# Latent mixers: u projected in pairs, convolution taps beside the projections, the second tile's heads behind the first search

## The chip, the cores and the metric

The kernel runs on one core of one Trainium2 chip. The metric is the device time of one execution in microseconds (us); lower is better. Times are medians of several executions. Everything is float32.

## What is computed

Two blocks of two layers each run one after the other on 256 tokens of width 1024. The change touches the second block only, and in it the two "latent" layers:

```
hx = modulate(x, sh1, s1)
q, k, v, u = split_cols(hx @ w_in[l])
q = apply_rope(rms(q.reshape(B, S, N_Q_HEADS, HEAD_DIM)) * q_gain[l], cos, sin)
k = apply_rope(rms(k.reshape(B, S, N_KV_HEADS, HEAD_DIM)) * k_gain[l], cos, sin)
o_attn = attend_latent(q, jnp.concatenate([kc, k], axis=1), jnp.concatenate([vc, v], axis=1))
o_conv = conformer_conv(u, conv_w[l], conv_b[l], ln_g[l], ln_b[l])
x = x + g1 * merge_groups(o_attn, o_conv, beta_attn[l], beta_conv[l], w_o[l])
x = x + g2 * peer(modulate(x, sh2, s2), peer_wq[l], peer_keys[l], peer_u[l], peer_v[l])
```

`conformer_conv` halves u (1024 columns) into a and gate, takes a * sigmoid(gate), and convolves its 512 channels along the tokens with 31 taps. `peer` picks, for each token and each of 8 heads, 16 of 16384 experts by two searches (best 16 of 128 keys twice, then best 16 of the 256 sums), gathers a row of u and a row of v for each pick, and adds up gelu(h . u) * weight * v.

## The kernel before, in words

Tokens lie in two tiles of 128 (t = 0, 1). Each engine runs one instruction stream written out by hand, and counts in semaphores order them. A latent layer (`stream_pe_in`, then `latent_mixer_pe`, `latent_mixer_act`, `latent_mixer_dve`, then a loop over 256 picks) goes so:

- PE projects q, k, v of both tiles (line 343 under a helper), then u as eight groups of 128 channels j = 0 to 7, where group j of a needs gate group j + 4. ACT reads each from PSUM (L995, identity or sigmoid). DVE meanwhile normalises and rotates q and k (L1303 to L1341) and signals `rot_ready`. PE transposes q and k (L337, "qk"), ACT copies them into `QT` and `KT`.
- DVE multiplies a by the gate in one instruction (L1345) into `PAD`. Then `maximum(i)` (L1436) finds the row maximum of head i's scores, and `taps_at(i)` gives the taps behind it. Each tap k of channel groups 0 to 2 is three DVE instructions (L1354, L1356) and a wait for the last of them (`link`). Group 3's taps are matmuls with diagonal matrices (L790), which POOL builds (L1223).
- The 16 heads (8 per tile) each go score (PE, L780), maximum (DVE), exponential (ACT, L1109), transposes (PE, L798), copy (ACT, L1117), values (PE, L807), with two buffers each. Heads 0 to 12 are begun beside the taps, and 13 to 15 beside the first search.
- Behind the taps: the convolution is transposed (L819), normalised, gated, multiplied by w_o (line 343), and gives h of tile 0 (L1481). PE projects queries and key scores of expert head 0 (L763), DVE searches (`search(0, 0)`, `search(0, 1)`) and writes the first 16 picks to `IDX` (L1650).
- From then on POOL fetches one row pair per pick (L2901), 1 MB each, into one of 15 slots. For pick n DVE takes the dot product (L2846), ACT the gelu and a scaled diagonal (L2787 to L2794), and PE adds the row (L2710). Only then is the slot free. `SLOT_FROM_TO` says for which picks a slot is in use, and in which order slots are first taken. Tables by n hang the rest of the layer (more queries, searches, tile 1's w_o products at n = 12 and 18) into this loop. `free` makes the first use of a slot wait for whoever held the memory, as here for the query and key buffer and for the buffer of the probabilities:

```
SLOT_QKT: [(s.groups_done, groups.of("score", TT * QH - 1))], SLOT_PROBS: [(s.groups_done, groups.of("pv", TT * QH - 1))],
```

Slots `W0A` and `W1A` (picks 24 and 25) wait for tile 1's w_o products in the same way, and POOL takes all fetches in order.

## Time and profile before

| what | us |
|---|---|
| median of 3 runs | 2952.42 |
| lowest, highest | 2946.86, 2974.02 |
| span of the profiled execution | 2910.0 |
| DVE busy in the span | 2101.8 (72%) |
| PE busy in the span | 2441.3 (84%) |
| bytes moved, mean rate | 1038.89 MB, 357 GB/s |

The span runs from the first to the last instruction on the core, so some 42 us of the time lie outside it. In it the first latent layer's projections begin near 1272 us and the second's near 2090 us. In the rows, a start time is counted from the beginning of the span, a bracket at the end holds the idle time of the engine before the instruction and what ended it, and xN is the number of instructions merged into the row. A float32 matmul or transpose shows as two matmul instructions.

### The profile page before, as it was taken

The numbers are of one execution on the slowest core, as the hardware profiler recorded it, in microseconds if no ns is written. First come the engines' busy times: TensorE is split into PE (matmuls) and PEld (weight loads), VectorE is DVE, ScalarE is ACT, GpSimd is POOL, SyncE is SP. The second block draws the span as 40 slices with busy tenths as digits, with TensorE's granted clock in tenths as the row PEclk, the third lists the DMA queues.
The fourth block names the chain that finished last, engine by engine and source line by source line (L and its number), as shares of the span: only waits on it lengthen the run. The fifth ranks groups of instructions, "written<-read, shape, count | busy, mean of one in ns | idle before, by whom it ended". The sixth has DMA issues, their size and how long they took to land.

```text
span 2910.0 us, 27822 instructions
## 1 busy us (share of the span) xinstructions
PE 2441.3 (84%) x8610; PEld 1389.1 (48%) x8610; DVE 2101.8 (72%) x4478; ACT 819.3 (28%) x2274; POOL 1124.6 (39%) x1121
## 2 busy tenths in 40 slices
PE   6996898978898999979798877768797988877876
PEld 3664364756546566656444333324375444332322
DVE  1659479878888978788587777765466977777654
ACT  1231111100012100013443433334324444433443
POOL 1100445766563676461143333334211334333332
PEclk9988897989997899989899899989998999999999
DMA  8348999999999999982499999999831999999997
GB/s 349 144 181 339 369 415 383 374 412 413 416 411 365 402 394 412 395 297 76 191 413 420 420 420 420 420 419 409 351 123 50 414 420 420 420 420 420 420 421 318
DMA packets 183478, 1038.89 MB, mean 357 GB/s; under 512 B 26971, under 2 KB 28978, under 8 KB 99876
## 3 DMA queue, kind: packets, MB, share of 16 engines
q0 software_dynamic: 147456, 805.37, 68.1%
q1 hardware_dynamic: 35292, 230.38, 19.9%
q8 instruction: 70, 1.15, 0.2%
q10 hardware_dynamic: 584, 1.36, 0.1%
q14 instruction: 76, 0.62, 0.1%
HBM read 1032.60 MB, written 4.44 MB: 356 GB/s over the span
## 4 chain that ended last, share of the span: by engine, by line
DMA 33%; PE 31%; DVE 21%; issue 6%; POOL 4%; ACT 3%; SPq 0%; ACTq 0%; DVEq 0%; POOLq 0%
PE PS L343 13%; DMA W<-in_peer_uv,IDX 12%; PE PS L2710 12%; DMA PROJ<-in_peer_uv,IDX 7%; DMA ROWS<-in_peer_uv,IDX 4%; DVE ROWS L1356 4%; DMA ROWS<-in_peer_uv,IDXV 3%; DMA ROWS<-in_peer_uv,COEF 3%; POOL ROWS L2539 2%; DVE ROWS L2331 2%; PE PS L2132 1%; PE PS L2142 1%; DMA ACC<-in_peer_uv,COEF 1%; PE PS L483 1%; DVE PROD L2344 1%
## 5 line engine op out<-in xcount | busy, mean ns | idle before, releaser
L2710 PE MATMUL PS<-W,SCALE 128*128 128x512 f32 x1120 | 539.7, 625 | 99.1 <-ACT SCALE L2794 99.0
L2846 DVE CUSTOM_DVE_ANT_0 W<-W,PS 128x1024 f32<-128x1024 f32 x280 | 337.9, 1219 | 213.5 <-DMA W<-in_peer_uv,IDX 212.9
L2901 POOL DMA_INDIRECT W<-in_peer_uv,IDX x280 | 267.8, 957 | 400.6 <-PE PS L2710 344.9
L2710 PEld LDWEIGHTS PS<-W,SCALE 128*128 128x128 f32 x1120 | 214.2, 199 | 406.0 <-issue 404.9
L2539 POOL DMA_INDIRECT ROWS<-in_peer_uv,IDX x159 | 170.0, 1069 | 366.4 <-DVE IDX L1653 150.5
L2132 PE MATMUL PS<-XT,W 128*128 128x256 f32 x1408 | 307.4, 379 | 0.0
L2132 PEld LDWEIGHTS PS<-XT,W 128*128 128x128 f32 x1408 | 267.8, 190 | 45.5 <-issue 10.1
L2787 ACT ACTIVATE DOT<-DOT 128x1 f32<-128x1 f32 x512 | 103.5, 202 | 602.8 <-DVE DOT L2846 595.9
L343 PE MATMUL PS<-W,XT 128*128 128x512 f32 (+2 forms) x576 | 220.6, 545 | 10.5 <-ACT XT L963 5.7
L343 PE MATMUL PS<-XT,W 128*128 128x128 f32 (+1 forms) x1344 | 218.6, 323 | 3.7 <-ACT XT L1076 3.7
L2794 ACT ACTIVATE SCALE<-C,COEF 128x128 f32<-128x128 f32 x512 | 205.6, 402 | 48.2 <-PE PS L2710 1.4
L343 PEld LDWEIGHTS PS<-XT,W 128*128 128x128 f32 x1344 | 201.0, 194 | 26.8 <-issue 6.7
L2331 DVE CUSTOM_DVE_ANT_0 ROWS<-ROWS,PS 128x1024 f32<-128x1024 f32 x118 | 139.8, 1217 | 42.7 <-DMA ROWS<-in_peer_uv,IDX 40.9
L343 PEld LDWEIGHTS PS<-W,XT 128*128 128x128 f32 x576 | 109.1, 200 | 119.9 <-issue 108.2
L2790 ACT ACTIVATE COEF<-DOT,WGT 128x1 f32<-128x1 f32 x512 | 150.8, 295 | 48.3 <-ACT DOT L2787 0.8
L343 PE MATMUL PS<-W,CT 128*128 128x512 f32 x320 | 150.2, 627 | 6.9 <-ACT CT L1127 4.2
L2901 POOL DMA_INDIRECT ROWS<-in_peer_uv,IDX x44 | 41.6, 946 | 224.2 <-DVE EI L1655 178.9
L2142 PE MATMUL PS<-W,PP 128*128 128x512 f32 x192 | 95.1, 653 | 29.9 <-DVE PP L2499 29.9
L2344 DVE SCALAR_TENSOR_TENSOR PROD<-ROWS,COEF,PROD 128x1024 f32<-128x1024 f32 x80 | 102.7, 1284 | 22.3 <-DMA ROWS<-in_peer_uv,COEF 14.8
L1356 DVE SCALAR_TENSOR_TENSOR ROWS<-ROWS,COLC 128x256 f32<-128x256 f32 x270 | 115.5, 482 | 2.1
L2710 PE MATMUL PS<-ROWS,SCALE 128*128 128x512 f32 x176 | 93.4, 657 | 26.2 <-ACT SCALE L2794 26.0
L2539 POOL DMA_INDIRECT ROWS<-in_peer_uv,COEF x80 | 91.5, 1144 | 43.5 <-DVE PROD L2344 22.4
(422 smaller groups left out, 4066.7 us busy)
## 6 DMA issues: line engine op xcount, KB each, us to landing
W<-in_w_up SPq DMA_DIRECT2D x44, 1024.0 KB, 12.2
W<-in_w_in SPq DMA_DIRECT2D x21, 2048.0 KB, 11.1
W<-in_w_mod SPq DMA_DIRECT2D x7, 4096.0 KB, 12.8
W<-in_w_down SPq DMA_DIRECT2D x22, 1024.0 KB, 8.1
W<-in_peer_wq SPq DMA_DIRECT2D x6, 2048.0 KB, 8.8
W<-in_w_o SPq DMA_DIRECT2D x6, 2048.0 KB, 9.5
W<-in_w_out SPq DMA_DIRECT2D x4, 2048.0 KB, 11.8
ROWS<-in_w_mod SPq DMA_DIRECT2D x5, 1024.0 KB, 12.2
```

The source lines that it names most:

```text
L343: ins = nc.tensor.matmul(PS[:, b, cols[0]:cols[1]], lhs(k), rhs(k), start=start and k == 0, stop=stop and k == n_k - 1)
L1356: ins = nc.vector.scalar_tensor_tensor(B["U"][:, j, :], B["PAD"][:, j, k:k + S], tap, B["U"][:, j, :], ALU.mult, ALU.add)
L2132: ins = nc.tensor.matmul(PS[:, 2 * r + half, j * S:(j + 1) * S], up_half(i, half)[:, k, j * P:(j + 1) * P], XT[:, k, :], start=(k == 0), s ...
L2142: ins = nc.tensor.matmul(PS[:, 4 + 2 * t + n, :], HG[r][:, j, t * P:(t + 1) * P], wslot(2 + r, 2, D)[:, j, n * 512:(n + 1) * 512], start=F ...
L2331: nc.vector.tensor_tensor_reduce(beside_slot(l, m), beside_slot(l, m), h, 1.0, 0.0, ALU.mult, ALU.add, DOT[:, 0, m:m + 1]).then_inc(beside ...
L2344: nc.vector.scalar_tensor_tensor(total, slot, coef, total, ALU.mult, ALU.add).then_inc(beside_used, 1)
L2539: nc.gpsimd.indirect_dma_start(beside_slot(l, n), None, one_by_one, bass.IndirectOffsetOnAxis(index[:, n % PICKS:n % PICKS + 1], 0),).then ...
L2710: ins = nc.tensor.matmul(PS[:, SUMS2[t] + h, :], SCALE[:, n % NSCALE, :], v_of(n)[:, h * 512:(h + 1) * 512], start=m == 0, stop=m == PICKS ...
L2790: nc.scalar.activation(COEF[:, t, one], DOT[:, t, one], ACT.Copy, scale=WGT[:, t, one]).then_inc(s.coef_ready, 1)
L2794: nc.scalar.activation(SCALE[:, n % NSCALE, :], ident, ACT.Copy, scale=COEF[:, t, one]).then_inc(s.scale_ready, 1)
L2846: nc.vector.tensor_tensor_reduce(u_of(n), u_of(n), h_of(t), 1.0, 0.0, ALU.mult, ALU.add, DOT[:, t, m:m + 1]).then_inc(s.rows_used, 1)
L2901: nc.gpsimd.indirect_dma_start(pair_slot(n), None, in_pairs, bass.IndirectOffsetOnAxis(IDX[:, t, m:m + 1], 0),).then_inc(pair_signal(fetch ...
```

## The change

In the latent layers, and there alone:

- PE projects u in the order 0, 4, 1, 5, 2, 6, 3, 7, so that a group and its gate come together, and puts the transposes of q and k behind the sixth group. ACT follows that order, and takes the root for q and k behind one u group in place of two.
- DVE multiplies group by group (`pad`), and does 26 taps ahead of the first maximum: 12 over groups 0 and 1, 14 over groups 0 to 2. Each tap is one instruction on one group. It waits for that group's previous tap, which was never the instruction just before it. The number of DVE taps stays 93.
- Only tile 0's heads (0 to 7) run beside the rest of the taps, in pairs. Tile 1's heads (8 to 15) come behind the first search: their first four maxima lie between the search and pick 0, the others behind picks 0 and 1. ACT and PE do them ahead of pick 0.
- The slots of the query and key buffer and of the probabilities are first used by picks 7 and 8 in place of 4 and 5.

```diff
-(SLOT_ROWS, SLOT_G, SLOT_PROJ, SLOT_KV, SLOT_QKT, SLOT_PROBS, SLOT_W0B, SLOT_W1B, SLOT_W0A, SLOT_W1A,
- SLOT_W2A, SLOT_W2B, SLOT_W3A, SLOT_W3B, SLOT_MORE) = range(15)
-SLOT_FROM_TO = [(0, 72), (0, 180), (0, 256), (0, 180), (0, 256), (0, 180), (0, 256), (0, 256), (24, 256), (24, 256),
-                (76, 256), (76, 256), (76, 256), (76, 256), (0, 256)]
+(SLOT_ROWS, SLOT_G, SLOT_PROJ, SLOT_KV, SLOT_MORE, SLOT_W0B, SLOT_W1B, SLOT_QKT, SLOT_PROBS, SLOT_W0A, SLOT_W1A,
+ SLOT_W2A, SLOT_W2B, SLOT_W3A, SLOT_W3B) = range(15)
+SLOT_FROM_TO = [(0, 72), (0, 180), (0, 256), (0, 180), (0, 256), (0, 256), (0, 256), (0, 256), (0, 180), (24, 256), (24, 256),
...
 NSCALE = 4
-TAP_HEADS = 12
-
-
-def taps_at(i):
-
-    return range(TAPS2 * i // TAP_HEADS, TAPS2 * (i + 1) // TAP_HEADS)
+U_ORDER = (0, 4, 1, 5, 2, 6, 3, 7)
+QK_TURN = 6
+PE_GROUP = 3
+PE_TAPS = (0, 6, 12, 18, 24, TAPS2)
+
+
+def tap_plan(parts):
+
+    done, before, plan = [0] * PE_GROUP, None, []
+    for n, groups in parts:
+        plan.append([])
+        for _ in range(n):
+            free = [g for g in range(groups) if done[g] < TAPS2]
+            g = min(free, key=lambda g: (g == before, done[g], g))
+            plan[-1].append((g, done[g]))
+            done[g], before = done[g] + 1, g
+    assert done == [TAPS2] * PE_GROUP, done
+    return plan
+
+
+TAP_PLAN = tap_plan([(12, 2), (14, 3), (14, 3), (14, 3), (14, 3), (25, 3)])
...
-            for j in range(8):
+            def turn_queries():
+                pe.wait_ge(s.rot_ready, 1)
+                transposes(pe, s, banks, groups, "qk", lambda t, k: B["QR"][:, t, k * P:(k + 1) * P], 6, s.qkT_ready, 0)
+
+            for i, j in enumerate(range(8) if beside else U_ORDER):
                 c = 2 + j // 4
                 if j % 4 == 0:
                     weights_in(pe, s, c, first)
-                b = banks.take(s.conv_in_ready, j + 1)
+                if not beside and i == QK_TURN:
+                    turn_queries()
+                b = banks.take(s.conv_in_ready, i + 1)
                 matmul_rows(pe, b, (0, S), lambda k: wslot(c, DK, 512)[:, k, (j % 4) * P:(j % 4 + 1) * P],
                             lambda k: XT[:, k, :], DK).then_inc(s.groups_done, groups.mark("u", j))
                 groups.at["u", j, "bank"] = b
             if beside:
                 beside(banks, 0)
-
-            pe.wait_ge(s.rot_ready, 1)
-            transposes(pe, s, banks, groups, "qk", lambda t, k: B["QR"][:, t, k * P:(k + 1) * P], 6, s.qkT_ready, 0)
+                turn_queries()
             pe.wait_ge(s.qkT_ready, 3)
...
             banks.leave_out(5)
             banks.hold(5, s.conv_ready, 2)
-            for i in range(TAP_HEADS):
-                score(i)
-                taps(taps_at(i))
-                if i >= 2:
+            for i in range(0, QH + 2, 2):
+                if i < QH:
+                    score(i)
+                    score(i + 1)
+                if i:
                     turn_probs(i - 2)
-                if i >= 3:
-                    sum_values(i - 3)
-            head(12)
+                    turn_probs(i - 1)
+                taps(range(PE_TAPS[i // 2], PE_TAPS[i // 2 + 1]))
+                if i:
+                    sum_values(i - 2)
+                    sum_values(i - 1)
             pe.wait_ge(s.conv_ready, 2)
...
+            banks.read_out[6] = (s.merged_ready, 1)
+            banks.banks, banks.i = [b for b in banks.in_turn() if b not in (2, 3)] + [6], 0
             turn_h(0)
             queries(0, 0)
             key_scores(0, 0)
-            for i in (13, 14, 15):
-                score(i)
             for c in range(2):
                 product("Y", 1, c, s.y_read, 2 + c + 1)
-            for j in (13, 14, 15):
-                turn_probs(j)
-                sum_values(j - 1)
-            sum_values(15)
             queries(0, 1)
             key_scores(0, 1)
-            banks.read_out[6] = (s.merged_ready, 1)
+            score(QH)
+            score(QH + 1)
+            for i in range(QH + 2, TT * QH + 2, 2):
+                if i < TT * QH:
+                    score(i)
+                    score(i + 1)
+                for j in (i - 2, i - 1):
+                    turn_probs(j)
+                for j in (i - 2, i - 1):
+                    sum_values(j)
...
-            exps(13)
...
                 nc.scalar.copy(H[:, 1, c * 512:(c + 1) * 512], PS[:, b, :]).then_inc(s.y_read, 1)
-            exps(15)
-            for j in (13, 14, 15):
-                probs_turned(j)
             queries_in(0, 1)
             scores_in(0, 1)
+            for i in range(QH, TT * QH + 2, 2):
+                if i == QH + 4:
+                    first_softmax()
+                if i > QH:
+                    probs_turned(i - 2)
+                    probs_turned(i - 1)
+                if i < TT * QH:
+                    exps(i)
+                    exps(i + 1)
...
+        def conv_for(dve, s, link, B):
+            step_of = {}
+
+            def pad(g):
+                dve.wait_ge(s.conv_in_ready, 2 * g + 2)
+                nc.vector.tensor_tensor(B["PAD"][:, g, HALO:HALO + S], B["U"][:, g, :], B["U"][:, 4 + g, :], ALU.mult).then_inc(s.pad_ready, 1)
+
+            def taps(part):
+                for g, k in part:
+                    tap = B["COLC"][:, g, k:k + 1]
+                    if k == 0:
+                        dve.wait_ge(s.pad_ready, g + 1)
+                        ins = nc.vector.tensor_scalar(B["U"][:, g, :], B["PAD"][:, g, 0:S], tap, B["COLC"][:, g, TAPS2:TAPS2 + 1], ALU.mult, ALU.add)
+                    else:
+                        dve.wait_ge(s.dve_step, step_of[g])
+                        ins = nc.vector.scalar_tensor_tensor(B["U"][:, g, :], B["PAD"][:, g, k:k + S], tap, B["U"][:, g, :], ALU.mult, ALU.add)
+                    ins.then_inc(s.dve_step, 1)
+                    step_of[g] = link.count.next()
+
+            def taps_done():
+                dve.wait_ge(s.dve_step, link.count.value())
+                dve.sem_inc(s.conv_ready, 1)
+
+            return pad, taps, taps_done
         def context_mixer_dve(dve, s, link, norms, groups, B, SRC):
...
-            for i in range(TAP_HEADS):
+            pad(0)
+            pad(1)
+            taps(TAP_PLAN[0])
+            pad(2)
+            taps(TAP_PLAN[1])
+            pad(PE_GROUP)
+            for i in range(0, QH, 2):
                 maximum(i)
-                for k in taps_at(i):
-                    tap_step(k)
-            maximum(12)
+                maximum(i + 1)
+                taps(TAP_PLAN[2 + i // 2])
+            taps_done()
             merge_heads(0)
...
                     maximum(i)
-            return {"key": last_maxima}, {
-                2: second_heads, 3: second_stat, 7: second_ratio, 16: lambda: add_product("O", 1, 0, ri[:, 0, 2:3]),
+            return {
+                -2: lambda: second_maxima(QH), -1: lambda: second_maxima(QH + 2), 0: lambda: second_maxima(QH + 4),
...
-                    within["key"]()
                     search(0, 1)
+                    later[-2]()
+                    later[-1]()
                     for n in range(TT * PICKS):
                         t, m = divmod(n, PICKS)
```

On PE, from the end of the projections of u of a latent layer into the heads (XT,W is u, C,QR the transposes of q and k, QKT a score, the rows with CT are taps of group 3, C,ROWS and V,ROWS probabilities and values). Before:

```order
L343 MATMUL PS<-XT,W 128x256 x64
L337 MATMUL PS<-C,QR 128x128 x12
L780 MATMUL PS<-QKT 128x512
L790 MATMUL PS<-ROWS,CT 128x256 x2
L780 MATMUL PS<-QKT 128x512
L790 MATMUL PS<-ROWS,CT 128x256 x3
L780 MATMUL PS<-QKT 128x512
L790 MATMUL PS<-ROWS,CT 128x256 x2
L798 MATMUL PS<-C,ROWS 128x128 x4
```

After:

```order
L358 MATMUL PS<-XT,W 128x256 x48
L352 MATMUL PS<-C,QR 128x128 x12
L358 MATMUL PS<-XT,W 128x256 x16
L799 MATMUL PS<-QKT 128x512 x2
L809 MATMUL PS<-ROWS,CT 128x256 x6
L799 MATMUL PS<-QKT 128x512 x2
L817 MATMUL PS<-C,ROWS 128x128 x8
L809 MATMUL PS<-ROWS,CT 128x256 x6
L826 MATMUL PS<-V,ROWS 128x64 x8
```

The transposes of q and k moved ahead of the last two u groups, and scores come two at a time.

On DVE, from the last copy of k and v into the heads. Before:

```order
L1341 COPY V<-KV 128x256
L1345 TENSOR_TENSOR ROWS<-ROWS 128x4x256
L1436 TENSOR_REDUCE NMAX<-PS 128x1
L1354 TENSOR_SCALAR ROWS<-ROWS,COLC 128x256 x3
L1356 SCALAR_TENSOR_TENSOR ROWS<-ROWS,COLC 128x256 x3
L1436 TENSOR_REDUCE NMAX<-PS 128x1
L1356 SCALAR_TENSOR_TENSOR ROWS<-ROWS,COLC 128x256 x9
```

After:

```order
L1366 COPY V<-KV 128x256
L1394 TENSOR_TENSOR ROWS<-ROWS 128x256 x2
L1401 TENSOR_SCALAR ROWS<-ROWS,COLC 128x256 x2
L1404 SCALAR_TENSOR_TENSOR ROWS<-ROWS,COLC 128x256 x10
L1394 TENSOR_TENSOR ROWS<-ROWS 128x256
L1401 TENSOR_SCALAR ROWS<-ROWS,COLC 128x256
L1404 SCALAR_TENSOR_TENSOR ROWS<-ROWS,COLC 128x256 x13
L1394 TENSOR_TENSOR ROWS<-ROWS 128x256
L1486 TENSOR_REDUCE NMAX<-PS 128x1 x2
L1404 SCALAR_TENSOR_TENSOR ROWS<-ROWS,COLC 128x256 x14
```

Twenty-six taps now stand ahead of the first maximum.

On DVE, from the first picks to the first row's dot product (ISA is the dot product, its second row the accumulator). Before:

```order
L1650 TENSOR_SCALAR IDX<-EI,BASE 128x16
L1655 TENSOR_TENSOR EI<-BV 128x16
L2846 ISA ROWS,DOT<-ROWS,PS 128x1024
L2846 ISA DOT 128x1
L1663 TENSOR_REDUCE SUM<-EI 128x1
```

After:

```order
L1707 TENSOR_SCALAR IDX<-EI,BASE 128x16
L1712 TENSOR_TENSOR EI<-BV 128x16
L1486 TENSOR_REDUCE NMAX<-PS 128x1 x4
L2903 ISA ROWS,DOT<-ROWS,PS 128x1024
L2903 ISA DOT 128x1
L1486 TENSOR_REDUCE NMAX<-PS 128x1 x2
L1720 TENSOR_REDUCE SUM<-EI 128x1
```

The maxima of tile 1's heads are behind the picks. Before, three stood between the two halves of the search, and the others beside the taps.

## Rows read from the trace of the kernel before

**Rows 1.** The page: shares of the chain of waits by engine.

```profile
DMA 33%; PE 31%; DVE 21%; issue 6%; POOL 4%; ACT 3%; SPq 0%; ACTq 0%; DVEq 0%; POOLq 0%
```

**Rows 2.** Busy time by stretch: us, PE, PEld, DVE, ACT, POOL, PE clock, DMA share, GB/s.

```profile
1320.80:1369.50 48.70, 44.47 (x212) 30.29 (x213) 47.58 (x106) 14.58 (x36) 7.70 (x12) 0.97 0.12 41
1480.00:1500.00 20.00, 20.00 (x72) 10.81 (x71) 18.93 (x51) 7.75 (x23) 11.39 (x11) 1.00 0.99 397
...
2280.00:2300.00 20.00, 20.00 (x49) 8.46 (x48) 19.24 (x54) 7.78 (x28) 8.44 (x9) 0.97 1.01 422
```

**Rows 3.** Timeline of DVE, first latent layer: start, us, what.

```profile
1318.01 1.23 DVE L1345 TENSOR_TENSOR ROWS<-ROWS 128x1024 f32<-128x1024 f32 x1 [4.53 <-ACT ROWS L995]
...
1322.67 1.39 DVE L1356 SCALAR_TENSOR_TENSOR ROWS<-ROWS,COLC 128x256 f32<-128x256 f32 x3
...
1340.56 1.27 DVE L1356 SCALAR_TENSOR_TENSOR ROWS<-ROWS,COLC 128x256 f32<-128x256 f32 x3
...
1340.56 1.79 DVE L1356 SCALAR_TENSOR_TENSOR ROWS<-ROWS,COLC 128x256 f32<-128x256 f32 x4
...
1365.13 3.89 DVE L1356 SCALAR_TENSOR_TENSOR ROWS<-ROWS,COLC 128x256 f32<-128x256 f32 x9
```

**Rows 4.** Timeline of DVE, second latent layer.

```profile
2124.73 0.28 DVE L1236 RECIPROCAL ri<-rt 128x20 f32<-128x20 f32 x1 [4.04 <-ACT rt L954]
...
2145.25 1.23 DVE L1345 TENSOR_TENSOR ROWS<-ROWS 128x1024 f32<-128x1024 f32 x1 [9.85 <-ACT ROWS L995]
...
2194.98 1.28 DVE L1356 SCALAR_TENSOR_TENSOR ROWS<-ROWS,COLC 128x256 f32<-128x256 f32 x3
```

**Rows 5.** Timeline of PE, both latent layers.

```profile
2117.01 27.79 PE L343 MATMUL PS<-XT,W 128*128 128x256 f32 x128
2144.63 1.47 PE L337 MATMUL PS<-C,QR 128*128 128x128 f32 x12
...
1319.64 1.12 PE L780 MATMUL PS<-QKT 64*128 64x512 f32 x2 [0.78 <-ACT QKT L1006]
...
1360.89 1.56 PE L790 MATMUL PS<-ROWS,XT 128*128 128x256 f32 x6
1362.29 0.60 PE L798 MATMUL PS<-C,ROWS 128*128 128x128 f32 x4
1362.73 1.00 PE L807 MATMUL PS<-V,ROWS 128*128 128x64 f32 x8
...
2231.36 1.89 PE L780 MATMUL PS<-QKT 64*128 64x512 f32 x6
...
1373.19 8.94 PE L343 MATMUL PS<-W,CT 128*128 128x512 f32 x16 [1.23 <-ACT CT L1127]
...
2200.43 7.13 PE L343 MATMUL PS<-W,CT 128*128 128x512 f32 x16 [1.23 <-ACT CT L1127]
```

**Rows 6.** Timelines of DVE, ACT and POOL around the first search, first latent layer.

```profile
1407.23 0.49 DVE L1548 MAX8 TV<-ROWS 128x8 f32<-128x128 f32 x2 [8.13 <-ACT ROWS L1090]
...
1410.46 1.89 DVE L1436 TENSOR_REDUCE NMAX<-PS 128x1 f32<-128x512 f32 x3
...
1424.88 1.22 DVE L2846 CUSTOM_DVE_ANT_0 ROWS<-ROWS,PS 128x1024 f32<-128x1024 f32 x1 [5.90 <-DMA ROWS<-in_peer_uv,IDX]
...
1445.27 1.21 DVE L2846 CUSTOM_DVE_ANT_0 ROWS<-ROWS,PS 128x1024 f32<-128x1024 f32 x1
...
1411.18 0.69 ACT L1109 ACTIVATE ROWS<-PS,NMAX 128x512 f32<-128x512 f32 x1 [1.76 <-DVE NMAX L1436]
...
1418.12 0.59 ACT L1117 COPY ROWS<-PS 128x512 f32<-128x512 f32 x1 [0.33 <-PE PS L798]
...
1419.18 1.00 POOL L2901 DMA_INDIRECT ROWS<-in_peer_uv,IDX  x1 [90.68 <-DVE EI L1655]
...
1483.11 0.94 POOL L2901 DMA_INDIRECT W<-in_peer_uv,IDX  x1 [6.17 <-PE PS L343]
```

82 lines of the change are left out of this document (38 added, 44 removed).

## The prediction

> **What bounds the kernel.** I read the page's chain of waits first [rows 1]: DMA holds 33% of it, PE 31%, DVE 21%. The question is then which of them sets the end of the two stretches that the change touches, so I read busy time by stretch, and then the timelines.
>
> In the loop over picks it is the DMA: between 2280 and 2300 it moves 422 GB/s at a share of 1.01 [rows 2]. One row pair is 1.049 MB, so 2.5 us, and 256 of them take 640 us. Whatever DVE, PE or ACT save inside this loop is worth nothing unless a fetch is late. The layer ends when the last row is in, and so everything that starts the first fetch earlier is worth its full time, once per layer.
>
> Ahead of the first fetch the DMA is idle, and the end is set by DVE: from 1320.8 to 1369.5 it is busy 47.58 of 48.7 us, with PE close behind at 44.47 [rows 2]. Before that DVE waits: in the first latent layer 4.53 us between its last q/k step and the product a * gate [rows 3], in the second 9.85 us, and 4.04 us for ACT's root [rows 4]. The reader should see that the taps fill the stretch, and that they could have started before the last u group was in.
>
> **First latent layer, up to the end of the taps.** DVE comes free at 1318.01 - 4.53 = 1313.48 and is busy without a break from 1298.6 to there, so the earlier root brings nothing here. The work behind it, by the new order:
> - Four products of 256 columns. None is in the trace. Below lies nothing shorter than a quarter of the 1024-column one, 1.23 / 4 = 0.31; above lies a tap, about 0.40. I take 0.35: 1.4 us.
> - 93 taps. Three in a row take 1.27 us, a fourth behind a `link` brings it to 1.79 [rows 3]. So the step over the link is 0.52, and the two others, with a last one of 0.48, are 0.395 each. With 9 taps and their links in 3.92 us (from this start to the next maximum) the mean before is 0.435. In the new order the instruction waited for is two or three back, hence long done, and I take 0.395: 36.7 us. If the step stays at the mean, 40.5 us.
> - POOL builds its diagonals meanwhile: three taps then take 1.39 in place of 1.27 [rows 3], 0.04 each, for some 25 taps: 1.0 us.
> - 8 maxima of 0.61 (three in 1.89, the last of them 0.69 [rows 6]) in place of 13: 4.9 us.
>
> Sum 44.0: the taps end at 1357.5, against 1365.13 + 3.89 = 1369.02 [rows 3]. **Gain 11.5 us**, or 7.7 if the links' time stays.
>
> Does anything else end later? PE takes 3.45 us for a u group (27.79 / 8 [rows 5]), so the sixth is done near 1310.8. There it waits for `rot_ready` until 1313.5 with the last two groups queued behind, and then needs 1.5 for the transposes and 6.9 for the groups: scores from 1322.0. DVE reaches its first maximum at 1313.5 + 1.4 + 26 x 0.395 + about 0.5 = 1325.7. So the wait has 2 to 3 us of cover. Behind it, a round of PE is a pair of scores, two transposes (0.44 each), six taps (0.47 each) and two value products (0.93 each). A lone score takes 1.05, but the three in a row took 1.82 together [rows 5], because neighbouring heads lie in different halves of the rows: I take 1.0 a pair. That is 6.6 us, against 7.0 on DVE (two maxima and 14 taps). PE's rounds end near 1325.7 + 2.8 + 3 x 6.6 + 6.0 = 1354.3, 3 us ahead of DVE. It is covered, but narrowly.
>
> **Second latent layer.** Here DVE is early: the root comes 3.3 us sooner (behind one u group), q and k are done at 2132.1, the products and 26 taps wait for u groups, and the last comes from PE. PE's groups and the transposes end at 2117.01 + 27.8 + 1.3 = 2146.1 [rows 5]; ACT's sigmoid takes 0.5 and DVE's product 0.35: 2147.0. Behind that stand 8 maxima and 67 taps: 4.9 + 26.5 + 1.0 = 32.4, so 2179.4, against 2194.98 + 1.28 = 2196.26 [rows 4]. **Gain 16.9 us**, or 14.2 if the links' time stays. The earlier root is not needed for it: with q and k at 2135.4 the 26 taps would still end before 2147.
>
> **From the taps to the first fetch.** The w_o products, h, the queries and the key scores stay, and PE and ACT bound them; the heads taken out (10 to 12) stood beside them. One price is open, the clock. PE's first 16 matmuls there took 8.94 us in one layer and 7.13 in the other [rows 5], and PE now waits 3 us ahead of them where before it waited 1 to 2. Between nothing and 1.8 us per layer, I take 0.9 for the second layer, and leave the first as it was.
>
> The three maxima between the two halves of the search go: 1410.46 to 1412.26, 1.8 us [rows 6]. How much of it lasts depends on the fetches. Fetch n, issued later than 2.5 n us after the first one, leaves the DMA idle. Pick 25's was issued at 1483.11, 63.9 us after 1419.18 [rows 6], so 1.4 late, and the stretch shows it: 397 GB/s between 1480 and 1500 [rows 2]. It waits for the second tile's w_o product, which stands behind 18 rows on PE, and that queue is bound by DVE's second search, done at 1445.27 [rows 6].
>
> Where is that search in the new order? Count from the start of the first search, Z (1407.23). The picks are ready at 9.9 and fetched from 10.1 (was 11.95); row 0 lands 5.7 later. PE ends the w_o products, the queries and key scores at 9.2 and then has heads 8 and 9. A pair of heads is scores 1.0, exponentials 1.4, transposes 0.9, copies 1.1, values 1.9 [rows 5, 6], and two pairs overlap. Followed instruction by instruction, the fourth pair's values end at Z + 25.8. DVE needs them for the merge behind row 2, which it reaches at 26.0. Its second search then ends at Z + 37.2, against 38.0 before. ACT and PE, who cannot touch row 0 before Z + 25, make it up: rows 0 to 4 are on PE by 38.8, and row 5 could not come before 39. Slots: picks 7 and 8 get theirs at Z + 19.8 and 25.8, wanted at 27.6 and 30.1. So pick 25's fetch comes 0.8 earlier, not 1.85. I keep 0.9 per layer: **1.8 us**.
>
> **Sum.** 11.5 + 16.9 + 1.8 - 0.9 = 29.3 us. The profiled span of 2910.0 would become 2881. What lies outside it is not touched, so from the median 2952.4 I get 2923. A measurement tells about 1% of this kernel, 29.5 us, from no change, so the forecast stands right on that line.
>
> One rule speaks against a term. The Trainium skill's page "VectorE: DVE Perf Modes", section "The DRAIN you can't avoid", says that chained DVE operations drain whether or not a semaphore stands between them, so that only the number of operations counts. The rows differ: 0.395 without a wait, 0.52 with one. By the page the taps stay at their mean.
>
> **Rivals.**
> - *The links' time stays*, because a wait on each tap costs as much as one on every third. For it: 93 waits now, where there were 31. Against it: the three maxima each wait for a semaphore and still follow at 0.6 us, less than their own 0.69 [rows 6]. Price 3.8 + 2.7 = 6.5: 2930. Chance 0.08.
> - *The heads starve the fetches.* Eight heads behind the search hold ACT and PE back from row 0, and each us by which their end passes Z + 25.8 delays DVE's merge, the second search, and pick 25's fetch. With no overlap a pair takes 7.5 us, and the four end near Z + 39: 13 us per layer, 26 in all. Half of that gives 2936, all of it 2949. For it: two buffers each for probabilities and their transposes, and DVE's maxima queued behind rows that have yet to land. Chance 0.14.
> - *Slower: PE's clock falls and stays.* In the first latent layer PE now waits 2.7 us for `rot_ready` and 2 to 3 more for the fourth product, just ahead of the rounds. If the granted clock (0.97 over the taps before [rows 2]) stayed at 1.2 of 2.4 GHz, the 28.6 us of PE's rounds would be 57, 25 us past DVE's end in each layer: 29 - 50 is 21 us slower, 2973. It costs something once the slow stretch is longer than about 6 us, and makes the kernel slower if it holds for some three quarters of both stages. Against it: PE is over 90% busy in the rounds. Chance 0.05.
> - *It does less than it says*: the early taps find no idle time in the first layer (counted so above), and a late u group or diagonal takes it in the second too. Then only the five maxima and the links are saved, 7 + 6, with 2: 2938. Chance 0.05.
>
> **How the numbers follow.** The forecast, with 2 to 4 us on either side for the clock (0 to 3.6), the products (0.6) and the second search, has 0.68 and covers 2915 to 2931; just under half of it is past the line. Of the slower side of the remaining cases I keep all but the last few us of starvation and the clock case. Range 2912 to 2944. Faster by over 1%: 0.38. Slower by over 1%: 0.06. Within 1%: 0.56.
>
> **What would show it.** In the profile of the changed kernel: taps of about 0.395 from start to start, with none of 0.52; their last one 11 to 17 us nearer to the first u group; no DVE idle ahead of the first maximum in the first latent layer, and in the second idle only at the third and fourth product; pairs of scores of 1.0 us; no maximum between the halves of the first search; pick 25's fetch 64 to 65 us behind the first. The prediction is wrong if PE's clock in the rounds is far below 0.97, if DVE waits long for a score, or if the DMA falls below 400 GB/s in the first 40 us of fetching.

## The result, and the profile of the changed kernel

| | before | changed |
|---|---|---|
| median of 20 runs, us | 2948.89 | 2936.63 |
| lowest, us | 2932.98 | 2916.09 |
| ratio, with its 95% interval | | 0.9947 (0.9926 to 0.9969) |
| span of the profiled execution, us | 2910.0 | 2953.7 |

The ratio says 15.6 us faster (9.1 to 21.8), half of the 29.3 us that were forecast. A second timing gave 0.9945 (0.9924 to 0.9965). One run of the 20, 3737.03 us, was disturbed and is left out of the ratio.

The changed kernel's profiled span is longer than that of before although the kernel is faster, so the two spans must not be set against each other. The first block, which the change doesn't touch, took 62 us longer in this execution; some 50 of them are two slow stretches of PE, of which the profile of before has none (the last section has the rows). And hardly anything lies outside a span: this execution took 2955.51 us at 2953.7 of span, so the 42 us that I counted as lying outside it are in truth the distance between a quick execution and a usual one. No timed run of the kernel before was shorter than 2925.85 us. So I compare stretches that begin and end at the same instruction.

The chain of waits of the changed kernel, shares by engine, beside [rows 1]:

```profile
PE 33%; DMA 31%; DVE 20%; issue 7%; POOL 5%; ACT 4%; another core or an unknown queue 0%; SPq 0%; ACTq 0%; DVEq 0%; POOLq 0%
```

**Up to the end of the taps.** DVE's timeline, first latent layer of the changed kernel, beside [rows 3]:

```profile
1375.07 0.29 DVE L1366 COPY V<-KV 128x256 f32<-128x256 f32 x1
1375.50 0.77 DVE L1394 TENSOR_TENSOR ROWS<-ROWS 128x256 f32<-128x256 f32 x2
1376.18 0.73 DVE L1401 TENSOR_SCALAR ROWS<-ROWS,COLC 128x256 f32<-128x256 f32 x2
1376.82 4.05 DVE L1404 SCALAR_TENSOR_TENSOR ROWS<-ROWS,COLC 128x256 f32<-128x256 f32 x10
...
1387.05 1.28 DVE L1486 TENSOR_REDUCE NMAX<-PS 128x1 f32<-128x512 f32 x2
...
1408.84 9.97 DVE L1404 SCALAR_TENSOR_TENSOR ROWS<-ROWS,COLC 128x256 f32<-128x256 f32 x25
```

No row of this stage has a bracket, those left out included: the 4.53 us of idle time are gone. Ten taps take 4.05 us and 25 take 9.97, so (9.97 - 0.47) / 24 = 0.396 from start to start. The last tap ends at 1418.81, 43.45 us behind the last q/k step (1375.36), against 1369.02 - 1313.48 = 55.54 before.

The same in the second latent layer, beside [rows 4]:

```profile
2172.95 0.28 DVE L1261 RECIPROCAL ri<-rt 128x20 f32<-128x20 f32 x1 [0.58 <-ACT rt L971]
...
2190.02 0.43 DVE L1394 TENSOR_TENSOR ROWS<-ROWS 128x256 f32<-128x256 f32 x1 [0.87 <-ACT ROWS L1025]
...
2198.24 0.43 DVE L1394 TENSOR_TENSOR ROWS<-ROWS 128x256 f32<-128x256 f32 x1 [2.19 <-ACT ROWS L1025]
2198.87 1.29 DVE L1486 TENSOR_REDUCE NMAX<-PS 128x1 f32<-128x512 f32 x2 [0.21 <-PE PS L799]
...
2220.93 9.97 DVE L1404 SCALAR_TENSOR_TENSOR ROWS<-ROWS,COLC 128x256 f32<-128x256 f32 x25
```

The root's wait fell from 4.04 to 0.58 us, and 9.85 us of idle time became 0.87 + 2.19 at the third and fourth product. From the first q/k step (2169.36) to the last tap it is 61.55 us, against 78.57.

**Behind the search.** PE in the changed kernel, both layers, beside [rows 5] (W,CT is tile 1's w_o product, QKT scores, V,ROWS values, SCALE the first row):

```profile
1454.71 9.48 PE L358 MATMUL PS<-W,CT 128*128 128x512 f32 x16
...
1466.66 1.89 PE L799 MATMUL PS<-QKT 64*128 64x512 f32 x8
...
1483.74 2.00 PE L826 MATMUL PS<-V,ROWS 128*128 128x64 f32 x16 [0.24 <-ACT ROWS L1139]
1486.66 3.65 PE L2767 MATMUL PS<-ROWS,SCALE 128*128 128x512 f32 x4 [0.92 <-ACT SCALE L2850]
...
2266.22 7.13 PE L358 MATMUL PS<-W,CT 128*128 128x512 f32 x16
...
2275.82 1.89 PE L799 MATMUL PS<-QKT 64*128 64x512 f32 x8
...
2288.09 2.96 PE L826 MATMUL PS<-V,ROWS 128*128 128x64 f32 x16 [4.08 <-ACT ROWS L1139]
...
2298.34 2.00 PE L826 MATMUL PS<-V,ROWS 128*128 128x64 f32 x16 [0.24 <-ACT ROWS L1139]
```

DVE and POOL in the changed kernel's first latent layer, beside [rows 6]:

```profile
1455.28 0.49 DVE L1605 MAX8 TV<-ROWS 128x8 f32<-128x128 f32 x2 [8.13 <-ACT ROWS L1112]
...
1475.56 1.29 DVE L1486 TENSOR_REDUCE NMAX<-PS 128x1 f32<-128x512 f32 x2 [2.82 <-PE PS L817]
...
1465.43 1.00 POOL L2958 DMA_INDIRECT ROWS<-in_peer_uv,IDX  x1 [67.26 <-DVE EI L1712]
...
1472.95 0.93 POOL L2958 DMA_INDIRECT W<-in_peer_uv,IDX  x1 [0.31 <-issue]
1479.67 0.94 POOL L2958 DMA_INDIRECT QKT<-in_peer_uv,IDX  x1 [5.78 <-PE PS L799]
...
1534.87 0.94 POOL L2958 DMA_INDIRECT W<-in_peer_uv,IDX  x1 [6.16 <-PE PS L358]
```

The first fetch comes 10.15 us behind the search's start in place of 11.95. But the heads end at 1485.74, 30.5 us behind it, and pick 25 is fetched at 1534.87, 69.4 us behind the first fetch in place of 63.9. Busy time of 20 us of each layer's gather, beside [rows 2]:

```profile
1526.00:1546.00 20.00, 20.00 (x56) 9.48 (x56) 18.40 (x42) 8.77 (x29) 10.57 (x11) 1.00 0.97 363
2340.00:2360.00 20.00, 20.00 (x53) 9.14 (x52) 18.60 (x43) 9.10 (x31) 9.83 (x11) 1.00 0.96 369
```

363 and 369 GB/s stand where before, at the same distance from the first fetch, there were 397 and 393. And it is not only there: the DMA is short of rows much sooner. From 20 to 40 us behind the first fetch, the two layers before and then the two layers of the changed kernel:

```profile
1439.20:1459.20 20.00, 16.55 (x66) 9.26 (x65) 15.16 (x53) 9.85 (x26) 4.30 (x5) 0.83 1.01 421
2264.00:2284.00 20.00, 15.51 (x65) 8.71 (x64) 15.17 (x53) 9.86 (x25) 4.48 (x5) 0.91 1.01 422
```

```profile
1485.40:1505.40 20.00, 17.95 (x71) 10.04 (x70) 15.60 (x41) 13.54 (x35) 7.00 (x7) 0.91 0.92 349
2297.40:2317.40 20.00, 17.05 (x79) 10.29 (x77) 16.90 (x44) 13.67 (x29) 7.00 (x7) 1.00 0.87 326
```

Pick 8 goes into the slot of the probabilities, which is free only when the heads end; its fetch came 0.6 and 3.2 us later than 2.5 us a row allows. Pick 9 goes where row 0 was, and row 0 reaches PE only 0.9 us behind the heads' end; it came 2.6 and 3.6 us late, where before it was 10 us early. The DMA waits there and further on, and that is where half of the gain went back.

### The profile page after: what moved, and what is told of

Its sections match the earlier page's. It is cut to its first block, busy times and chain, and to the rows that moved or that the text cites. A ratio compares the mean times of both kernels' runs of the same rounds, so it can differ in the third digit from the quotient of the medians.

```text
span 2953.7 us, 27804 instructions
## 1 busy us (share of the span) xinstructions
PE 2450.4 (83%) x8610; PEld 1393.7 (47%) x8610; DVE 2097.9 (71%) x4484; ACT 819.0 (28%) x2274; POOL 1122.8 (38%) x1121
## 4 chain that ended last, share of the span: by engine, by line
PE 33%; DMA 31%; DVE 20%; issue 7%; POOL 5%; ACT 4%; another core or an unknown queue 0%; SPq 0%; ACTq 0%; DVEq 0%; POOLq 0%
PE PS L358 15%; PE PS L2767 11%; DMA W<-in_peer_uv,IDX 6%; DMA QKT<-in_peer_uv,IDX 5%; DMA MORE<-in_peer_uv,IDX 4%; DMA ROWS<-in_peer_uv,IDXV 4%; DMA G<-in_peer_uv,IDX 3%; POOL ROWS L2596 3%; DVE ROWS L1404 2%; DVE ROWS L2388 2%; DMA ROWS<-in_peer_uv,COEF 2%; DMA KV<-in_peer_uv,IDX 2%; DMA PROJ<-in_peer_uv,IDX 1%; PE PS L2199 1%; DMA MORE<-in_peer_uv,COEF 1%
## 5 line engine op out<-in xcount | busy, mean ns | idle before, releaser
L2189 PEld LDWEIGHTS PS<-XT,W 128*128 128x128 f32 x1408 | 268.6, 191 | 49.3 <-issue 13.7
L358 PE MATMUL PS<-W,XT 128*128 128x512 f32 (+2 forms) x576 | 240.2, 572 | 40.8 <-issue 33.5
L2401 DVE SCALAR_TENSOR_TENSOR PROD<-ROWS,COEF,PROD 128x1024 f32<-128x1024 f32 x80 | 102.7, 1284 | 23.6 <-DMA ROWS<-in_peer_uv,COEF 13.7
L2767 PE MATMUL PS<-PROJ,SCALE 128*128 128x512 f32 x176 | 92.5, 651 | 29.4 <-ACT SCALE L2850 29.3
L358 PEld LDWEIGHTS PS<-W,CT 128*128 128x128 f32 x320 | 63.8, 203 | 90.9 <-issue 81.5
```

Of the source, the lines that this page charges most:

```text
L358: ins = nc.tensor.matmul(PS[:, b, cols[0]:cols[1]], lhs(k), rhs(k), start=start and k == 0, stop=stop and k == n_k - 1)
L2189: ins = nc.tensor.matmul(PS[:, 2 * r + half, j * S:(j + 1) * S], up_half(i, half)[:, k, j * P:(j + 1) * P], XT[:, k, :], start=(k == 0), s ...
L2401: nc.vector.scalar_tensor_tensor(total, slot, coef, total, ALU.mult, ALU.add).then_inc(beside_used, 1)
L2767: ins = nc.tensor.matmul(PS[:, SUMS2[t] + h, :], SCALE[:, n % NSCALE, :], v_of(n)[:, h * 512:(h + 1) * 512], start=m == 0, stop=m == PICKS ...
```

## The stretches in every kernel

All profiles are cut at the same instructions, in us. "Taps": in the first latent layer from the last q/k step, in the second from the first one, to the last tap. "Search": from there to the first search. "Fetch": from the search to the first fetch. "Heads' end": end of the last value product, from the search. "Pick 25": its fetch, from the first one. "Gather": from the first fetch to the second layer's first q/k step, and to the end of the span. "Sum" adds taps, search, fetch and gather of both layers. Each cell has the two layers. (The expectations end the first layer's gather where the second's projections begin, 28.2 us sooner: their 670.3 is the 698.5 here.)

| kernel | taps | search | fetch | heads' end | pick 25 | gather | sum |
|---|---|---|---|---|---|---|---|
| before | 55.5, 78.6 | 38.2, 35.8 | 11.95, 11.95 | 13.9, 13.7 | 63.9, 64.0 | 698.5, 666.0 | 1596.5 |
| changed | 43.5, 61.5 | 36.5, 35.9 | 10.15, 10.6 | 30.5, 33.6 | 69.4, 72.3 | 703.9, 676.3 | 1578.3 |
| again | 43.4, 61.6 | 35.9, 38.3 | 10.2, 10.6 | 30.7, 30.7 | 69.6, 69.5 | 703.6, 672.6 | 1576.2 |
| link | 48.4, 64.0 | 36.0, 38.1 | 10.2, 10.6 | 31.8, 28.4 | 70.8, 67.2 | 707.1, 670.0 | 1584.5 |
| late taps | 54.7, 71.6 | 38.5, 35.3 | 10.15, 10.6 | 31.7, 30.7 | 70.6, 69.5 | 707.0, 672.5 | 1600.3 |
| u order | 46.5, 63.6 | 38.3, 38.3 | 10.2, 10.6 | 30.3, 30.7 | 69.3, 69.5 | 700.2, 672.6 | 1580.3 |
| 10 heads | 44.6, 62.9 | 36.0, 34.7 | 10.2, 10.6 | 29.4, 24.9 | 68.5, 63.6 | 701.3, 666.2 | 1566.5 |
| 10 heads again | 44.6, 62.9 | 35.3, 35.9 | 10.2, 10.6 | 26.1, 29.2 | 66.4, 68.1 | 702.6, 671.2 | 1573.3 |
| 12 heads | 48.5, 64.4 | 34.7, 35.1 | 10.2, 10.6 | 22.7, 21.7 | 63.1, 64.3 | 698.3, 667.0 | 1568.7 |
| early pair | 43.5, 61.5 | 38.7, 36.5 | 10.2, 10.6 | 30.8, 33.1 | 70.1, 72.1 | 705.2, 674.6 | 1580.7 |
| 10 heads, early pair | 44.7, 62.9 | 34.7, 35.3 | 10.15, 10.6 | 25.9, 28.3 | 65.0, 67.3 | 698.2, 672.1 | 1568.6 |
| product at 14 | 44.2, 61.6 | 38.1, 36.5 | 10.2, 10.6 | 36.1, 30.9 | 72.8, 66.7 | 711.8, 672.0 | 1584.9 |
| product at 14, 10 heads | 45.9, 62.9 | 37.9, 35.3 | 10.2, 10.6 | 26.1, 26.5 | 64.0, 63.7 | 704.2, 668.9 | 1575.9 |

A stretch with the same code repeats to 0.1 us up to the taps' end (changed, again), to some 3.5 us on the way to the search, and to 3 to 4 us in the gather. A difference smaller than that, read there from one profile, shows nothing.

## Experiments

**The changed kernel once more.** No edit.

> The changed kernel once more, to have a second profiled execution of it. Theory A (the heads behind the first search hold up the rows, and pick 25's fetch with them): the stretch from the first fetch to the layer's end is 5 to 10 us longer than before in both layers (before 670.3 and 666.0), and pick 25 is fetched 69 to 72 us behind the first, in this execution too. Theory B (that was one execution's bad luck): one of the two stretches is back at 666 to 670. Up to the first fetch both expect what the first profile showed, 90.1 us behind the last q/k step in the first layer and 108.0 us behind the first q/k step in the second. Time: 0.995 of before by both.

Measured: 0.9945 (0.9924 to 0.9965). Both gathers are long again, by 5.1 and 6.6 us over before, and pick 25 comes at 69.6 and 69.5. The gain came back with the stretches ahead of the first fetch, and so did the give-back. Theory B falls.

**A wait behind every third tap.**

```diff
                     step_of[g] = link.count.next()
+                    step_of["n"] = step_of.get("n", 0) + 1
+                    if step_of["n"] % 3 == 0:
+                        dve.wait_ge(s.dve_step, step_of[g])
```

> The taps keep their order, but behind every third one DVE also waits for that tap itself, as it did before the change. If a wait on the instruction just issued is what cost 0.52 against 0.395 us, 31 of them cost 31 x 0.125 = 3.9 us in the first layer; in the second the 26 early taps have idle time beside them, so 22 x 0.125 = 2.8 us. Together 6.6 us, 0.2% of the time: less than the timing shows clearly, so it is read from the trace: the 14 taps between two pairs of maxima take about 6.3 in place of 5.7 us, and the taps end 3.9 us later behind the last q/k step (43.45 before this edit). If every chained tap drains anyway, the stretches stay at 5.7 us and nothing is later.

Measured: 0.9965 (0.9949 to 0.9981), and taps that end 5.0 and 2.5 us later. DVE's last taps of that kernel's first latent layer:

```profile
1377.98 10.97 DVE L1404 SCALAR_TENSOR_TENSOR ROWS<-ROWS,COLC 128x256 f32<-128x256 f32 x25
```

25 taps with eight such waits take 10.97 us where they took 9.97: 0.125 us for a wait on the instruction just issued, as forecast, and 0.11 for the second layer (2.5 / 22). The first layer's 5.0 us are 1.1 more than 31 x 0.125; the last section says what else slows taps there. The Trainium skill's page "VectorE: DVE Perf Modes", in "The DRAIN you can't avoid", says of eight copies that a semaphore behind each of them costs nothing extra. For these short taps the rows differ.

**The 26 early taps behind the first two maxima.**

```diff
-            pad(0)
-            pad(1)
-            taps(TAP_PLAN[0])
-            pad(2)
-            taps(TAP_PLAN[1])
-            pad(PE_GROUP)
+            for g in range(PE_GROUP + 1):
+                pad(g)
             for i in range(0, QH, 2):
                 maximum(i)
                 maximum(i + 1)
+                if i == 0:
+                    taps(TAP_PLAN[0])
+                    taps(TAP_PLAN[1])
                 taps(TAP_PLAN[2 + i // 2])
```

> As changed, but the 26 taps that stand ahead of the first maximum stand behind the first two, where PE's scores are awaited; the number of taps, waits and heads is the same. If the gain of the taps' stage comes from the idle time that these taps fill, it goes: in the first layer the scores are there 8.5 to 9.6 us behind the last q/k step, so the stage becomes some 8 us longer (43.4 to 51 or 52), and in the second, where the last u group bounds, 10.3 us longer (61.5 to 72 behind the first q/k step). Together 18 us, so no faster than before the change. If it comes from fewer maxima and waits (the rival that it does less than it says), the stage changes by less than 3 us in either layer.

Measured: 0.9987 (0.9970 to 1.0004). The taps end 11.2 and 10.1 us later, in the first layer 3 us more than expected, and the idle time is there again, in one row of DVE's timeline:

```profile
1360.95 0.43 DVE L1394 TENSOR_TENSOR ROWS<-ROWS 128x256 f32<-128x256 f32 x1 [10.72 <-ACT ROWS L1025]
```

So the early taps are worth 21 of the 29 us that the taps' stages gained. The rest, five maxima a layer, the links and the earlier root, is 8 us, where the rival "it does less than it says" counted 13; in the first layer it is 0.9.

**u in the old order.**

```diff
-U_ORDER = (0, 4, 1, 5, 2, 6, 3, 7)
+U_ORDER = tuple(range(8))
...
-                dve.wait_ge(s.conv_in_ready, 2 * g + 2)
+                dve.wait_ge(s.conv_in_ready, g + 5)
```

> As changed, but u is projected in the order of before, 0 to 7, with the transposes of q and k behind the eighth group, and each product waits for its own gate group. In the second layer the gates 4 to 7 come 3.45 us apart, the first some 3 us behind the last q/k step in place of 7 us ahead of it: the 26 taps then run in 13 us from 187 to 200 us on the trace's clock, while the first score is there near 199. Pairing then brings 1 to 3 us in the second layer and, with the transposes later and the fourth product at the same place, 0 to 2 us in the first. If pairing is what lets the taps start early at all, the stages grow by more than 5 us each.

In the kernel as it ran the transposes stayed behind the sixth group; only the order of the groups changed. Measured: 0.9948 (0.9932 to 0.9963), no different from the changed kernel, and in the trace 3.0 and 2.1 us of the taps' stage. Of the 3.0 us, DVE waits 1.54 for the third product's group, and the first 14 taps behind the maxima take 7.23 us in place of 5.89 for another reason (the last section). The pairing is the small part of this change; placing taps ahead of the maxima is the large one.

**How many heads beside the taps.** With HB heads there and 16 - HB behind the search, the loops of PE and ACT likewise; for ten:

```diff
-PE_TAPS = (0, 6, 12, 18, 24, TAPS2)
+HB = 10
+PE_TAPS = (0, 5, 10, 15, 20, 25, TAPS2)
...
-TAP_PLAN = tap_plan([(12, 2), (14, 3), (14, 3), (14, 3), (14, 3), (25, 3)])
+TAP_PLAN = tap_plan([(12, 2), (14, 3), (12, 3), (12, 3), (12, 3), (12, 3), (19, 3)])
...
-            for i in range(0, QH, 2):
+            for i in range(0, HB, 2):
                 maximum(i)
...
-                -2: lambda: second_maxima(QH), -1: lambda: second_maxima(QH + 2), 0: lambda: second_maxima(QH + 4),
+                -2: lambda: second_maxima(HB), -1: lambda: second_maxima(HB + 2), 0: lambda: second_maxima(HB + 4),
```

> Twelve heads beside the taps in pairs, and only heads 12 to 15 behind the first search; all else as changed. Theory A: the stretch from the first fetch to the layer's end goes back to 670 and 666 us (5.6 and 10.3 us less than in the changed kernel), pick 25 at 64 us; but PE now bounds the taps' stage: six pairs of heads at 4.1 us and 31 taps at 0.46 are 39 us, which start 8.5 us behind the last q/k step and end near 48 in the first layer (43.5 with eight heads), so some 5 us are lost again in each layer. Net 0 to 10 us faster than the changed kernel. Theory C (the give-back comes from the shorter list of early slots, not from the heads): the stretches stay at 676, and the kernel is some 10 us slower than the changed one, no faster than before.

Measured with twelve: 0.9932 (0.9892 to 0.9973). Both gathers are back at 698.3 and 667.0 with the same list of slots, pick 9 is 5.5 and 6.9 us early, and from 20 to 40 us behind the first fetch the DMA moves 421 and 420 GB/s. So theory C falls and theory A stands. And PE bounds the taps, as three rows like this one of DVE say (0.73 us of waiting for a score in each of the last rounds of the first layer):

```profile
1366.29 1.29 DVE L1487 TENSOR_REDUCE NMAX<-PS 128x1 f32<-128x512 f32 x2 [0.73 <-PE PS L800]
```

> Ten heads beside the taps, six behind the first search. From the traces of eight and of twelve heads: the taps end 43.5 and 48.5 us behind the last q/k step in the first layer; PE's queue passes DVE's near ten, so 45 to 46 is expected. Behind the search a pair costs 4 us: pick 25 about 66 to 67 us behind the first fetch. Time between those of eight and twelve heads or up to 4 us better than both.

Measured with ten: 0.9909 (0.9883 to 0.9936). The taps end only 1.2 and 1.4 us later than with eight heads, which is the price of two more maxima: PE is not yet the bound. Pick 25 comes at 68.5 in one layer and 63.6 in the other, around the 66 to 67 expected and too far apart to be called met.

> Ten heads beside the taps once more, to time it on one chip with the two others and to see how much its stretches vary: taps end 44.6 us behind the last q/k step in the first layer, pick 25 between 63.6 and 68.5 us behind the first fetch, following the end of the heads by 39.2 us. Ratio to before 0.991.

Measured: 0.9933 (0.9914 to 0.9952), and pick 25 at 66.4 and 68.1.

**One pair begun ahead of the search.** On PE (the maxima, exponentials and copies accordingly):

```diff
+            score(QH)
+            score(QH + 1)
             turn_h(0)
             queries(0, 0)
             key_scores(0, 0)
-            for c in range(2):
-                product("Y", 1, c, s.y_read, 2 + c + 1)
+            turn_probs(QH)
+            turn_probs(QH + 1)
+            product("Y", 1, 0, s.y_read, 2 + 1)
+            sum_values(QH)
+            sum_values(QH + 1)
+            product("Y", 1, 1, s.y_read, 2 + 2)
+            score(QH + 2)
+            score(QH + 3)
             queries(0, 1)
             key_scores(0, 1)
-            score(QH)
-            score(QH + 1)
```

> As changed, but the first pair of tile 1's heads (8, 9) is begun ahead of the search, where PE waits 7.3 us for h and DVE 8.1 us for the first scores: scores ahead of h's transposes, maxima behind h, exponentials behind the copy of h, transposes and values around tile 1's product. Theory A: one pair less behind the search ends the heads 4 to 5 us sooner, the second search and pick 25 come as much sooner, and the stretch from the first fetch to the end becomes about 671 us in both layers; nothing ahead of the first fetch moves by more than 1 us. Together 8 to 12 us faster than the changed kernel. Theory C: the stretches stay at 676 us, and so does the time.

Measured: 0.9943 (0.9925 to 0.9962), and heads that end no sooner, 30.8 and 33.1 us. The edit did what it says, but PE then ran the three other pairs at the lower of its two clocks for much of the way. Busy time and granted clock over 18 us, first of this kernel, then of the changed one (its second profile) at the same distance from the search:

```profile
1434.00:1452.00 18.00, 16.45 (x79) 11.60 (x76) 7.60 (x19) 7.20 (x20) 7.55 (x8) 0.72 0.87 345
```

```profile
1431.00:1449.00 18.00, 14.31 (x90) 9.99 (x87) 10.50 (x32) 10.37 (x25) 7.56 (x8) 0.91 0.87 343
```

16.45 us busy for 79 matmuls against 14.31 for 90. One product of values took 3.68 us where it takes 2.00. The exponentials of heads 10 and 11 also stood behind the copies of the second queries, which cost some 2 us more. Why the clock fell lower here was not tried.

> Ten heads beside the taps, the pair 10 and 11 begun ahead of the first search (scores ahead of h's transposes, maxima behind h, exponentials behind the copy of h), four heads behind the search, with the exponentials of 12 and 13 ahead of the copies of the second queries. Expected: taps end near 45 in the first layer (48.5 with twelve), the way from there to the search as in the run with the early pair (36 to 38.7), pick 25 at 63 to 64.5 us as with twelve heads, so 3 us better per layer than twelve heads: ratio to before 0.991. If PE's clock falls behind the search, as it did in the run with the early pair (0.72 over 18 us against 0.91), pick 25 comes near 67 and the gain over twelve heads is gone.

Measured: 0.9923 (0.9896 to 0.9950). Its sum of stretches equals that of twelve heads; one layer has pick 25 at 65.0, the other at 67.3. Not the 3 us a layer that were expected. The granted clock behind the search was 0.85 and 0.83 over 18 us, between the 0.72 and the 0.91 above, and ACT stalled in both layers (last section).

**The second half of tile 1's product behind row 14.**

```diff
-                    18: lambda: second_product(1), 24: lambda: queries(0, 3), 27: lambda: key_scores(0, 3), 33: lambda: turn_h(1),
+                    14: lambda: second_product(1), 24: lambda: queries(0, 3), 27: lambda: key_scores(0, 3), 33: lambda: turn_h(1),
```

> As changed, but the second half of tile 1's w_o product, whose weights lie where pick 25 lands, stands on PE behind row 14 in place of row 18: four rows of 1.88 us, 7.5 us, sooner. If only pick 25 is late, its fetch comes up to 7 us sooner and the layer's gather 4 to 7 us: 8 to 14 us for the kernel. If the whole queue is late, as picks 15 to 24 say (in the changed kernel's first layer pick 21 was issued 4.9 us later than 2.5 us a row allows, pick 15 3.6), the latest pick is then 21 at 4.9 in place of 25 at 6.9, and the gain is 2 us a layer, 4 us in all.

Measured: 0.9953 (0.9935 to 0.9971). In the second layer, whose heads ended as in the run "again" (30.9 and 30.7), pick 25 comes 2.8 us sooner, but pick 23 is then 6.7 us later than 2.5 us a row allows, where pick 25 had been 7.0: the gather is 0.6 us shorter. The whole queue of rows is late, and pick 25 is only where it shows most. In the first layer the heads ended 5.5 us later than elsewhere, by the stall that the last section shows, so that layer tells nothing of the edit.

> Both: ten heads beside the taps and the second half of the product behind row 14. With the heads ended 1 to 6 us sooner the queue is less late, so the same move brings 1 to 2 us a layer at most over ten heads alone, which is below what the timing shows; in the trace pick 25 is no longer the latest pick.

Measured: 0.9915 (0.9896 to 0.9934), between the two runs of ten heads. Pick 25 is no longer the latest (pick 23 is, by 4.0 and 3.7 us), and the gathers are no shorter than with ten heads alone.

## Why the prediction was half right

**The taps' stage: right, to 0.6 us.** Forecast gains 11.5 and 16.9 us, measured 12.1 and 17.0. The step of 0.395 us without a wait on the last instruction was 0.396, and the link's 0.125 us was confirmed by putting it back. That PE's rounds would stay just ahead of DVE's was right with eight heads (DVE never waits for a score in the first layer), and wrong in what it suggested: "covered, but narrowly" (PE's last values ended 2.2 us ahead of the last tap) still left room for one pair more, as the run with ten heads shows.

**The clock ahead of the search: of no account.** I took 0.9 us of loss. The stretch changed by -1.7 and +0.1 us in one profile and by -2.3 and +2.6 in the other; that is its spread.

**The search: right, 1.8 and 1.35 us** up to the first fetch, of which I kept 0.9 a layer because pick 25 would set the end.

**The heads behind the search: the step that failed.** It was "the fourth pair's values end at Z + 25.8", Z being the search's start. They ended at Z + 30.5 and 33.6, and at 30.7 twice in the second profile. How pick 25 hangs on that end was right: the walk put pick 25 at 75.9 - 0.8 = 75.1 behind Z, 49.3 behind the heads' end, and in the 18 layers of the table (without those of the product at 14) in which the heads end 24.8 us or more behind the search, pick 25 less heads' end is 49.1 to 50.5. Below that, with twelve heads (50.6, 53.2) and before (61.9, 62.2), something else comes last. So each us by which the heads passed 25.8 was paid in full: for heads 4.7 and 7.8 us late, pick 25 came at Z + 79.6 and 82.9, 4.5 and 7.8 us late. The gathers grew by 5.4 and 10.3, and by 5.1 and 6.6 in the second profile. One of the signs that I had named for a wrong prediction is there too: below 400 GB/s in the first 40 us of fetching. In its last 20 us it tells the two kernels apart (349 and 326 against 421 and 422); the first 20 us are below 400 before the change as well (360 and 366), so that half of the sign was badly chosen.

Why they ended late has three parts, and the rows show each. The first is the walk itself, which had 16.6 us from the first score to the last value. Twelve layers ran four pairs behind the search with this order of work. In the six of them whose product ran slowly (the second part, below) the pairs took 19.1 to 19.6 us, and in the one layer with neither that nor the stall of the third part (the second of "link") 19.3, ending at Z + 28.4. Over the first layer's pairs PE was busy 16.2 of 19.0 us, where the walk's pairs have 4 x 3.8 = 15.2 of it; the other 2.8 us it waited for ACT's exponentials and copies. The walk added up durations, and left little for the handing over from engine to engine.

The second part is the clock. The product ahead of the pairs took 9.48 us in place of 7.13, so the pairs began at Z + 11.4 and not 9.2; the granted clock over it was 0.75. In the second layer it took 7.13, and they did begin at Z + 9.0:

```profile
1454.71:1464.19 9.48, 9.48 (x20) 4.24 (x19) 8.30 (x34) 1.94 (x4) 0.00 (x0) 0.75 0.01 2
2266.22:2273.35 7.13, 7.13 (x20) 3.30 (x19) 6.12 (x29) 1.94 (x4) 0.00 (x0) 1.00 0.01 2
```

The third is a stall. In the second layer the pairs took 24.5 us: PE waits 4.08 us among them, which no work of theirs explains, and behind that wait the values take 2.96 us in place of 2.00. Of the six layers of the twelve whose pairs began at Z + 9.0, five have this stall; of the six that began at Z + 11.1 or later, none. So a layer had the one mishap or the other, and the heads ended at 30.3 to 30.9 with the slow product and at 30.7 to 36.1 with the stall.

**The sum.** 12.1 + 1.7 + 1.8 - 5.4 = 10.2 us in the first layer, 17.0 - 0.1 + 1.35 - 10.3 = 8.0 in the second: 18.2 us by these two profiles, 20.3 by the second one (1596.5 - 1576.2), 15.6 by the timing. That is the rival "the heads starve the fetches" at half its price, 2936. The ranking was wrong and its share of 0.14 too low: I had seen that the walk ended 0.2 us ahead of the point from which each us counts, and gave it no error of its own. Nothing was left of the links' rival or of the one that the change does less than it says. The clock's rival looked at the wrong place: PE kept its clock in the taps' rounds (0.94 and 1.00 over 30 us of them) and lost part of it behind the search.

**What is better.** Ten heads beside the taps: 0.9909, 0.9933 and, with the product moved, 0.9915, against 0.9947 and 0.9945 for eight. These intervals touch or overlap. But all four profiles with ten heads there have a lower sum (1566.5 to 1575.9) than the two of the changed kernel (1578.3, 1576.2), and with the product moved, timed on one chip, ten heads (0.9896 to 0.9934) lie just clear of eight (0.9935 to 0.9971). Twelve heads (0.9932, sum 1568.7) can't be told from ten.

## What to carry to other kernels

When work is moved out from beside a bound engine into a stretch with slack, the slack has to be compared with the spread of the moved work's end, not with a sum of durations: in the twelve layers with eight heads behind the search this chain of short steps over three engines ended 2.6 to 10.3 us later than the sum said, and in none of them on time. Find by one experiment how many pieces still fit beside the bound engine (here one pair more, for 1.3 us) before the rest is moved. A wait on the instruction just issued costs a third of a short instruction; interleaving independent chains takes it away without taking an instruction away.
